# Twelve bias lines spread over 128 partitions: by one broadcast in DRAM, or by twelve matmuls

## The reference, cut to what matters

```python
rel = qpos[:, None] - kpos[None, :]
bias = rel_bias[t5_causal_bucket(rel)].astype(jnp.float32)     # rel_bias: (32, 4)
s = jnp.einsum('bqhcd,bkhcd->bhcqk', qi, k).astype(jnp.float32) * scale
s = s + bias.transpose(2, 0, 1)[None, :, None]
s = jnp.where((rel >= 0)[None, None, None], s, -1e30)
...
s_own = jnp.einsum('hqd,hld->hql', qi, k_own) * scale + table_t[:, rel_bucket(d_own)]   # rp_table: (32, 8)
```

## Time and profile before

| what | value |
|---|---|
| median of three runs | 1587.74 us |
| the profiled execution | 1584.54 us |
| its span in the trace | 1582.8 us |
| PE busy | 1540.8 us (97%) |
| DVE busy | 894.2 us (56%) |
| ACT busy | 556.4 us (35%) |
| POOL busy | 45.8 us (3%) |
| DMA | 148.95 MB, mean 94 GB/s |
| granted TensorE clock, mean | 0.991 of full speed |

### The profile page before, as it was taken

The page is one execution under the profiler, slowest core; times in us unless marked ns, Lnnn a source line. Parts: engine busy times, 40 slices in busy tenths (PEclk is TensorE's granted clock), DMA queues, the critical chain, the costliest instruction groups (busy, mean ns, idle before and its releaser), DMA issues.

```text
span 1582.8 us, 20491 instructions
## 1 busy us (share of the span) xinstructions
PE 1540.8 (97%) x7066; PEld 1242.8 (79%) x7066; DVE 894.2 (56%) x1396; ACT 556.4 (35%) x819; POOL 45.8 (3%) x28
## 2 busy tenths in 40 slices
PE   7999999999999999999999998899999999999996
PEld 6877778788888888888777876778878888888885
DVE  6736565576665555443546768966655652256432
ACT  5214444324433333333325444324443331122220
POOL 0000000000000000000000001410000000000000
PEclk9999999999999999999999999899999999999998
DMA  6522212223222222332231232203212332222221
GB/s 233 202 86 88 73 60 91 72 91 106 93 93 98 101 93 93 107 106 95 104 120 67 80 121 73 87 27 104 70 41 93 107 101 98 93 93 93 94 66 53
DMA packets 43014, 148.95 MB, mean 94 GB/s; under 512 B 4632, under 2 KB 5032, under 8 KB 42836
## 3 DMA queue, kind: packets, MB, share of 16 engines
q1 hardware_dynamic: 38688, 137.38, 25.6%
q10 hardware_dynamic: 4276, 10.89, 2.0%
HBM read 146.13 MB, written 6.06 MB: 96 GB/s over the span
## 4 chain that ended last, share of the span: by engine, by line
PE 66%; issue 25%; DVE 6%; ACT 1%; DMA 1%; DVEq 0%; POOLq 0%; POOL 0%; ACTq 0%
PE ps L1100 21%; PE ps L1102 20%; PE ps L1101 20%; DVE wl L686 1%; PE ps L1229 1%; DVE qe L1832 1%; DVE a L1845 1%; ACT wh L478 1%; DMA x<-x_dram 0%; DVE ke L1834 0%; PE ps L2192 0%; PE ps L1139 0%; DMA bias<-bias_lines 0%; ACT s L1398 0%; DVE x L2043 0%
## 5 line engine op out<-in xcount | busy, mean ns | idle before, releaser
L478 ACT ACTIVATE wh<-stage 128x1024 fp32r<-128x1024 f32 x255 | 270.1, 1059 | 582.9 <-PE ps L1102 582.2
L1100 PE MATMUL ps<-hh,wh 128*128 128x512 f32 x1096 | 441.4, 403 | 10.8 <-DVE hl L698 10.8
L1102 PE MATMUL ps<-hh,wl 128*128 128x512 f32 x1096 | 428.4, 391 | 0.0
L1101 PE MATMUL ps<-hl,wh 128*128 128x512 f32 x1096 | 428.0, 391 | 0.0
L686 DVE TENSOR_TENSOR wl<-stage,wh 128x1024 fp32r<-128x1024 f32 x247 | 302.1, 1223 | 195.6 <-ACT wh L478 195.4
L1100 PEld LDWEIGHTS ps<-hh,wh 128*128 128x128 f32 x1096 | 206.3, 188 | 66.7 <-issue 21.8
L1102 PEld LDWEIGHTS ps<-hh,wl 128*128 128x128 f32 x1096 | 206.2, 188 | 44.2
L1101 PEld LDWEIGHTS ps<-hl,wh 128*128 128x128 f32 x1096 | 206.6, 189 | 40.8 <-issue 1.9
L1102 PE MATMUL ps<-ah,wl 128*128 128x512 f32 x432 | 170.6, 395 | 0.0
L1100 PE MATMUL ps<-ah,wh 128*128 128x512 f32 x432 | 170.6, 395 | 0.0
L1101 PE MATMUL ps<-al,wh 128*128 128x512 f32 x432 | 170.6, 395 | 0.0
(11 more groups left out here) (320 smaller groups left out, 1929.2 us busy)
## 6 DMA issues: line engine op xcount, KB each, us to landing
stage<-stream_dram SPq DMA_DIRECT2D x255, 512.0 KB, 3.2
bias_lines<-bias_line ACTq DMA_DIRECT2D x1, 3840.0 KB
x<-x_dram ACTq DMA_DIRECT2D x4, 512.0 KB, 10.0
bias<-bias_lines ACTq DMA_DIRECT2D x4, 512.0 KB, 4.9
out_dram<-x SPq DMA_DIRECT2D x8, 256.0 KB, 2.1
bias<-bias_lines ACTq DMA_DIRECT2D x4, 256.0 KB, 2.9
mem<-mem_dram ACTq DMA_DIRECT2D x1, 1024.0 KB, 4.9
early<-early_dram SPq DMA_DIRECT2D x1, 512.0 KB, 11.5
```

Source lines behind the costliest of these rows:

```text
L478: A(b.wh[:, p.slot, :], b.stage[:, p.slot, :], ACT.Copy).then_inc(s.hi_ready, 1)
L1100: MM(out, wh, xh, start=start, stop=False, skip_group_check=True)
L1101: MM(out, wh, xl, start=False, stop=False, skip_group_check=True)
L1102: return MM(out, wl, xh, start=False, stop=stop, skip_group_check=True)
```

## The change

The table now comes from the host with each column repeated 128 times (32 x 1536 values). For each of the 12 heads one matmul with 128 equal columns writes the head's line into all 128 partitions of PSUM, in bank 4 and bank 5 by turns; from the third on each waits until ACT has copied the one two before it. ACT copies 12 times 128 x 512 into `lines`, which is now 128 x 12 x 640, and issues one transfer from SBUF into `bias_lines`. The intermediate DRAM buffer, the write to it, the wait for that write and the DRAM-to-DRAM transfer are gone. The contents of `bias_lines` are the same.

```diff
-    b.lines = at("lines", R(24), [LINE])
+    b.lines = at("lines", R(24), [12, LINE])
...
-    b.tables = at("tables", R(98), [HEADS])
+    b.tables = at("tables", R(98), [12 * P])
...
-    act.wait_ge(s.line_done, 1)
-    A(b.lines[0:HEADS, 0:T], b.ps[0:HEADS, 4, :], ACT.Copy).then_inc(s.line_copied, 1)
+    for h in range(12):
+        act.wait_ge(s.line_done, h + 1)
+        A(b.lines[:, h, 0:T], b.ps[:, 4 + h % 2, :], ACT.Copy).then_inc(s.line_copied, 1)
     act.wait_ge(s.lines_set, 1)
-    act.wait_ge(s.line_copied, 1)
-    act.dma_start(line_dram, b.lines[0:HEADS, :]).then_inc(s.lines_out, 16)
+    act.wait_ge(s.line_copied, 12)
+    act.dma_start(scratch.rearrange("h (p j) -> p h j", p=P), b.lines[:]).then_inc(s.lines_out, 16)
     hi(Panel(P_POOL + 1 + RING))
     act.wait_ge(s.lam_dots, 1)
     A(b.lam_e, b.lam_d, ACT.Exp).then_inc(s.lam_exps, 1)
-
-    act.wait_ge(s.lines_out, 16)
-    act.dma_start(scratch.rearrange("h (p j) -> h p j", p=P),
-                  line_dram.unsqueeze(1).to_broadcast([HEADS, P, LINE])).then_inc(s.lines_out, 16)
...
-    act.wait_ge(s.lines_out, 32)
+    act.wait_ge(s.lines_out, 16)
...
-    G.memset(b.lines[0:HEADS, T:LINE], NEG).then_inc(s.lines_set, 1)
+    G.memset(b.lines[:, :, T:LINE], NEG).then_inc(s.lines_set, 1)
...
     pe.wait_ge(s.line_in, 32)
-    MM(b.ps[0:HEADS, 4, :], b.tables[0:NB, :], b.onehot[0:NB, :], start=True, stop=True).then_inc(s.line_done, 1)
+    for h in range(12):
+        if h >= 2:
+            pe.wait_ge(s.line_copied, h - 1)
+        MM(b.ps[:, 4 + h % 2, :], b.tables[0:NB, P * h:P * h + P], b.onehot[0:NB, :], start=True,
+           stop=True).then_inc(s.line_done, 1)
...
-        "tables": tables,
+        "tables": np.repeat(tables, P, axis=1),
```

More of the change, by code:

```diff
@@ L40 @@
 NB = 32
-HEADS = 12
 LINE = 640
@@ L230, in build @@
     b = place(nc)
-    scratch = nc.dram_tensor("bias_lines", (HEADS, P * LINE), F32).ap()
-    line_dram = nc.dram_tensor("bias_line", (HEADS, LINE), F32).ap()
+    scratch = nc.dram_tensor("bias_lines", (12, P * LINE), F32).ap()
     with nc.Block() as block:
@@ L239, in _ @@
         def _(act):
-            scalar_program(nc, act, s, b, dram, scratch, line_dram)
+            scalar_program(nc, act, s, b, dram, scratch)
         @block.vector
@@ L454, in sync_program, with scalar_program @@
     sp.wait_ge(s.out_done, 16 * KT)
-def scalar_program(nc, act, s, b, dram, scratch, line_dram):
+def scalar_program(nc, act, s, b, dram, scratch):
     A = nc.scalar.activation
@@ L1172, in tensor_program @@
     pe.wait_ge(s.ws_masked, 1)
-    pe.wait_ge(s.line_copied, 1)
+    pe.wait_ge(s.line_copied, 12)
     for f in range(2):
```

## The result

| | before | after |
|---|---|---|
| median | 1586.14 us (1581.84 to 1592.82, 4 runs) | 1602.55 us (1601.19 to 1604.30, 4 runs) |
| ratio, after to before | | 1.0098, 95% interval 1.0080 to 1.0115 |
| span of the profiled execution | 1582.8 us | 1602.7 us |

What follows compares the result with a forecast made beforehand. PE was taken to bound the kernel, busy at full clock around the change. Removal gave 0 and eleven matmuls added 9.9 us to the median 1587.74, giving 1597.6 us; range 1593 to 1602, wider range 1591.0 to 1603.0.

Steps and rivals of the forecast that it cites:

- What bounds the kernel: Around the change PE is busy 219.94 of 220.00 us at clock 1.00, so each added PE instruction delays everything behind.
- What is removed: Small buffer's write, the wait for it and the DRAM-to-DRAM broadcast were all hidden, so removing them gives 0.
- Eleven matmuls of about 0.9 us, 9.9 in all: Eleven added 32-row line matmuls on PE make it 9.9 us later; bounds 9.5 to 13.0.
- the first of the three readings: In full use of the array, a float32 matmul of 512 columns costs PE 0.86 us, 0.43 a pass, whatever its rows.
- The prediction's own sign of being wrong: Wrong if line matmuls are spaced 1.1 us or more, span grows much less than the shift, or PE waits for DVE.
- rival 1: Each added line matmul pays a lone one's 1.18 us: 13.0 added, 1600.7 us; open weight loads 2.4; chance 0.12.
- The round with ACT, 1.81 us for two: Alternating PSUM banks: matmul, ACT copy, release and weight load take 1.81 us per two line matmuls, against PE's own 1.72.
- DVE's spare 3.3 us and the knock-on: Before panel 10, DVE has 3.3 us spare, 3.0 after ACT's longer issue, cost 0; any excess adds; chance 0.67 with forecast.
- The transfer, 14 to 32 us: The 3.93 MB write from SBUF ends between 75 and 93 us, read from 129.8 us: at least 37 spare, cost 0.
- The start: Larger table load, 196 KB, takes 0.7 us among early inputs and POOL's fill is 12 times wider: cost 0.
- Rival 2: PE and ACT in lockstep: each line matmul costs the whole 1.81 us, 19.9 added, 1607.6 us; chance 0.04.
- Rivals 3 and 4: 3: passes run side by side, 1592.9 us, chance 0.08; 4: DVE waits in linear attention swallow delay, 1587.7 us, chance 0.09.

Runs made afterwards that it cites:

- the direct transfer alone: Kernel before, with only the small DRAM buffer, its write and wait replaced by one SBUF transfer repeating each of 12 partitions' lines 128 times: 1585.36 us, ratio 1.0013.
- 128-row kernel: Changed kernel with each line matmul on 128 rows instead of 32, the table standing four times below itself: 1595.40 us, ratio 1.0065 to the kernel before.
- the twelve repeats: Kernel before, with its one 32-row, 12-column matmul issued twelve times in a row into the same bank, nothing else added: 1603.03 us, ratio 1.0105.
- spread kernel: Changed kernel with the twelve 32-row matmuls placed one before each tile step of panels 4 and 5, not in a row: 1611.91 us, ratio 1.0199.

## Why the prediction was right, and where it was not

The forecast of 1597.6 us is 5.0 below the measured 1602.55. It would be 6.5 below if the base had been the median of four (1586.14) instead of the median of three (1587.74): 1.6 us of the miss are hidden by a base that was too high. That the wider range held the time, by 0.45 us, is luck; 9.9 us were added in the forecast and 16.4 measured. Nor does the narrower range, 1593 to 1602, follow from the terms given for it, which make 1594.2 to 1603.7.

- *What bounds the kernel: right.* PE stayed without idle time around the change, and the delay at 72 us arrived at the end in full.
- *What is removed is worth 0: right*, by the direct transfer alone.
- *Eleven matmuls of about 0.9 us, 9.9 in all: mis-sized.* It measured 17.3 us for the line matmuls and 2.2 for the panel behind them in the first trace; in the second, 14.7 and 1.7. The step that failed is the first of the three readings, that "a pass streams 512 columns through the array whatever the table's width" and that half the rows change nothing. It holds at a given clock: 0.86 us between the first two copies with 32 rows, 1.71 at half of it. It does not hold for the clock, which I took as 1.00 from the earlier trace rows and carried over to a stretch of other work. With 128 rows the same step gives the measured delay on PE to within 0.2 us (9.7), and with 128 or 64 rows the medians are 10.6 and 10.9 us above those of before. The prediction's own sign of being wrong came, a spacing of 1.1 us or more, but it was tied to rival 1, whose 13.0 us and whose cause are not what was found.
- *The round with ACT, 1.81 us for two: right where the clock held* (0.86 and 0.95 in the 128-row kernel), and without effect in the changed one, where PE itself needs 1.71 us for each.
- *DVE's spare 3.3 us and the knock-on: right.* No wait of PE appears between 48 and 130 us. ACT's issue took 0.41 us, not 0.91.
- *The transfer, 14 to 32 us: a little pessimistic*, 12.9 us.
- *The start: right* but for the 0.22 us, for which no cause was found.
- *The rivals.* Rival 1's price for open weight loads did not come: two 32-row matmuls on the same rows are 0.86 us apart at full clock, no more than on the full array. The Trainium skill, "TensorE: Matmul & The Clock Gate", section The mechanism, has loads overlap only with matmuls on other rows; the trace does not agree for these. Rival 2's 1.81 us a matmul is near the 1.71 measured, and this is an accident: its cause, that PE and ACT don't overlap, is refuted by the twelve repeats, which are as slow with one copy behind them all, and by the 128-row kernel, which keeps 0.86 and 0.95 us beside the same twelve copies. Rivals 3 and 4 did not happen.

A hint at the rival that was missing stood in the trace of before. In the second block PE does 32 matmul passes of one column each, at 1042.28 us, between full ones. The timeline, then the windows of PE:

```profile
1042.28 3.63 PE L2212 MATMUL ps<-consts,gsq 128*128 128x1 f32 x32
1045.77 0.54 PE L1100 MATMUL ps<-yh,wh 128*128 128x512 f32 x1
1046.11 0.63 PE L1101 MATMUL ps<-yl,wh 128*128 128x512 f32 x1
1046.53 0.63 PE L1102 MATMUL ps<-yh,wl 128*128 128x512 f32 x1
```

```profile
1044.00:1046.00 2.00, 2.00 (x19) 1.00 0.00 0
1046.00:1048.00 2.00, 2.00 (x6) 0.51 0.04 8
1048.00:1050.00 2.00, 2.00 (x8) 0.64 0.00 0
```

PE is busy 2.00 of 2.00 us in each of these windows, and yet the full matmuls behind the small ones run 0.42 to 0.43 us apart at half clock. So behind a stretch of small matmuls this kernel had lost its clock before, with no idle time that a row shows. These passes are on 128 rows and of one column, so they are another case than the lines, and that they are the cause is argued, not tested; a row's end is also modelled, so that short gaps between them can't be ruled out. The changed kernel shows the same with matmuls of 512 columns, from 52 us on. The Trainium skill, "TensorE: Matmul & The Clock Gate", section Why this matters for your kernels, names only idle gaps of PE between bursts as what throws the clock back. These traces do not agree that gaps alone are to be feared, since by their rows PE has none.

## What to carry to other kernels

A row that says PE is busy says nothing about the clock. Before work of another shape is priced from full-array rows, look in the trace for a stretch of such work and read the granted clock there and behind it; without one, price it at both levels and keep both in the range. If matmuls with few rows must stand in a row, using more rows by repeating the operand, with each 1 of the one-hot matrix in one of the copies, cost nothing on PE and kept the clock, for a larger load at the start: 1596 instead of 1602 us. It is better still not to multiply PE's work to remove a transfer for which nobody waits.

## What was not expected of the hardware

- Twelve matmuls of 32 rows in a row took the clock to 0.50 with PE busy throughout, in all four traces of it; three to six of them ran at full clock first. With 64 and with 128 rows it stayed at 1.00, in one trace each. The number of result rows (12 or 128) made no difference to speak of (1603.0 and 1602.0 us).
- The clock was still low behind them, for twelve full-array matmuls (5.1 us) in the first trace of the changed kernel.
- The same program lost the clock in one execution and kept it in another (spread kernel: 1600.2 and 1611.2 us in the two traced).
- A transfer that repeats 12 partitions out of SBUF slowed panel loads beside it from 3.2 to 20.4 us in the median; the one from 128 partitions wrote the same 3840 KB in 12.9 us.
